# One fused two-layer kernel on one core: the opening, the compression tiles, the gated output and two norms reordered

## What is computed

```python
h = rmsnorm(x, norm_w)                                   # layer 1
proj = h @ w_in                                          # 16 column groups of 512 and more
kc, vc = compress(kc_raw, pe_k, w1_k, w2_k), compress(vc_raw, pe_v, w1_v, w2_v)
o = nsa_attention(q, kc, vc, ks, vs, kw, vw, gates)      # three branches, gated per head
y_b = (o * silu(g_nsa)) @ w_nsa_out
merged = gm[0] * y_a + gm[1] * y_b
x = rmsnorm(x + merged @ w_out, final_norm_w)
# layer 2: adaptive norm, attention a and b, gated merge
x = x + g1 * (merged @ w_out_2)
h2 = rms_norm(x, norm2_w) * (1 + sc2) + sh2
x = rms_norm(x + g2 * ff(h2), final_w)
```

## Time and profile before

| | |
|---|---|
| median of three runs | 2280.42 us (2279.46 to 2280.89) |
| profiled execution | 2282.75 us, its span 2281.1 us |
| TensorE busy | 2250.8 us, 99% of the span |
| VectorE, ScalarE, GpSimd busy | 1556.1, 1105.4, 149.9 us |
| data moved | 546.49 MB, 240 GB/s on average |
| share of TensorE in the chain that ended last | 87% |

### The profile page before, as it was taken

One profiled execution on the slowest core, in us unless ns is written; L12 is line 12 of the kernel. 1 busy time (PEld: TensorE's weight loads), 2 busy tenths in 40 slices (PEclk: granted clock), 3 DMA queues, 4 the chain that ended last, 5 costly groups with the idle time before them and its releaser, 6 DMA issues.

```text
span 2281.1 us, 31278 instructions
## 1 busy us (share of the span) xinstructions
PE 2250.8 (99%) x10377; PEld 1863.9 (82%) x10377; DVE 1556.1 (68%) x1936; ACT 1105.4 (48%) x1437; POOL 149.9 (7%) x285
## 2 busy tenths in 40 slices
PE   8999999999999999999999999999999999999998
PEld 6888888788788888888888888888888888888886
DVE  5685777777776556788777776666555666655566
ACT  6454445566564444533366554445444443444444
POOL 1000110000000000011011210000000000000000
PEclk9999999999999999999999999999999999999999
DMA  8887897555665766598588886666666666666564
GB/s 286 288 283 266 302 337 253 205 193 202 211 225 175 272 209 228 199 320 292 195 284 288 311 317 248 235 217 213 210 212 221 230 222 228 227 213 208 207 205 146
DMA packets 150104, 546.49 MB, mean 240 GB/s; under 512 B 17249, under 2 KB 17392, under 8 KB 148496
## 3 DMA queue, kind: packets, MB, share of 16 engines
q1 hardware_dynamic: 112400, 406.37, 51.4%
q0 software_dynamic: 34752, 129.71, 16.3%
q10 hardware_dynamic: 2880, 9.44, 1.0%
HBM read 534.92 MB, written 10.53 MB: 239 GB/s over the span
## 4 chain that ended last, share of the span: by engine, by line
PE 87%; DVE 6%; ACT 3%; issue 2%; DMA 2%; DVEq 0%; ACTq 0%; SPq 0%
PE ps L1805 22%; PE ps L1807 22%; PE ps L1806 22%; PE ps L1922 5%; PE ps L1924 5%; PE ps L1923 5%; DVE w_lo L1065 2%; PE ps L1844 2%; DMA raw<-ws_dram 2%; ACT prob L787 1%; ACT w_hi L619 1%; PE ps L1981 1%; PE ps L2028 1%; DVE prob L1226 1%; PE ps L1822 0%
## 5 line engine op out<-in xcount | busy, mean ns | idle before, releaser
L1065 DVE TENSOR_TENSOR w_lo<-raw,w_hi 128x1024 fp32r<-128x1024 f32 x761 | 927.8, 1224 | 617.5 <-ACT w_hi L619 599.7
L619 ACT ACTIVATE w_hi<-raw 128x1024 fp32r<-128x1024 f32 x753 | 795.7, 1061 | 996.5 <-PE ps L1807 859.8
L1805 PE MATMUL ps<-w_hi,a_hi 128*128 128x512 f32 x1632 | 638.6, 391 | 3.4 <-DVE w_lo L1065 1.7
L1807 PE MATMUL ps<-w_hi,a_lo 128*128 128x512 f32 x1632 | 636.2, 390 | 0.0
L1806 PE MATMUL ps<-w_lo,a_hi 128*128 128x512 f32 x1632 | 636.0, 390 | 0.0
L1805 PEld LDWEIGHTS ps<-w_hi,a_hi 128*128 128x128 f32 x1632 | 306.9, 188 | 67.1 <-issue 2.2
L1807 PEld LDWEIGHTS ps<-w_hi,a_lo 128*128 128x128 f32 x1632 | 306.9, 188 | 64.1
L1806 PEld LDWEIGHTS ps<-w_lo,a_hi 128*128 128x128 f32 x1632 | 307.1, 188 | 63.1
L1922 PE MATMUL ps<-w_hi,a_hi 128*128 128x512 f32 x640 | 258.5, 404 | 0.4 <-DVE w_lo L1065 0.4
L1924 PE MATMUL ps<-w_hi,a_lo 128*128 128x512 f32 x640 | 249.8, 390 | 0.0
L1923 PE MATMUL ps<-w_lo,a_hi 128*128 128x512 f32 x640 | 249.3, 390 | 0.0
(11 more groups left out here) (310 smaller groups left out, 2125.4 us busy)
## 6 DMA issues: line engine op xcount, KB each, us to landing
raw<-ws_dram SPq DMA_DIRECT2D x769, 512.0 KB, 4.2
ada<-wa_dram POOLq DMA_DIRECT2D x192, 512.0 KB, 4.8
gates_spill<-gst ACTq DMA_DIRECT2D x16, 512.0 KB, 5.4
ga<-gates_spill POOLq DMA_DIRECT2D x8, 512.0 KB, 4.2
gb<-gates_spill POOLq DMA_DIRECT2D x8, 512.0 KB, 6.0
bias_c<-b_merge_dram POOLq DMA_DIRECT2D x9, 256.0 KB, 4.9
x<-x_dram SPq DMA_DIRECT2D x4, 512.0 KB, 7.6
cb<-c_dram POOLq DMA_DIRECT2D x2, 1024.0 KB, 5.1
```

The costliest lines, as they stand in the source:

```text
L619: act.activation(w_hi[:, k.slot(RING), :], raw[:, k.slot(RING), :], ACT.Copy).then_inc(hi_done, 1)
L1065: dve.tensor_tensor(w_lo[:, k.slot(RING), :], raw[:, k.slot(RING), :], w_hi[:, k.slot(RING), :].bitcast(F32), ALU.subtract).then_inc(lo_do ...
L1805: pe.matmul(o, hi(m, tb), w_hi[:, s, cols], start=m == 0, stop=False)
L1807: mm = pe.matmul(o, lo(m, tb), w_hi[:, s, cols], start=False, stop=m == of * kts - 1)
```

## The change

There are four independent parts.

**1. Opening.** The identity and norm weights are one tensor `first`, issued by SP ahead of everything. The first weight tile comes in two halves, the first piece of x in two halves on ACT's queue. ACT runs a tiny activation first. TensorE runs 11 matmuls on zeros (128x128), then the first turn, then seven more, then the first tile in two halves with turn 1 between and turn 2 behind; ACT and DVE split the first tile in halves, after the first `a_hi` and `a_lo`.

**2. Compression tiles.** `cmp_w1_k` alternates with `vw`, `cmp_w1_v` with the second q projection (before it followed `vw`), in the order of `BESIDE`. The transposes of the hidden rows and the last products of the compression stand later.

**3. Gated output.** In each nsa group DVE makes the gated output of the third unit ahead of that step's splits. The modulation that stood ahead of the splits goes behind the `y_lo` of that unit.

**4. Norms.** Tiles 2 to 7 of the last output chunk are dealt by block, tile 3 from its ring slot, the other five from outside the ring. The split of the next stage's tile 3 waits until tile 3's second half is used.

```diff
+BESIDE = [(1, 0), (1, 1)] + [t for j in range(6) for t in ((0, j), (1, j + 2))] + [(0, 6), (0, 7)]
...
+        HELD = RING - 1
+        ASIDE = [j for j in range(T_K - len(spots["norm2"]) - 1, T_K) if j != HELD]
+        WHOLE = ASIDE[0]
...
+            sp.dma_start(first[:], t["first"]).then_inc(first_in, 16)
+            sp.dma_start(raw[:, 0, 0:NC], ws[0][:, 0:NC]).then_inc(raw0_in, 16)
+            sp.dma_start(raw[:, 0, NC:TW], ws[0][:, NC:TW]).then_inc(raw_landed[0], 16)
...
+            act.dma_start(x0[:, 0, :, 0:S], x_first[:, :, 0:S]).then_inc(x0_in, 16)
+            act.dma_start(x0[:, 0, :, S:NC], x_first[:, :, S:NC]).then_inc(x_in[0], 16)
...
                 last_squares(name, 0)
                 std(name, 0)
+                split_after(At(kp + HELD), kp - T_K + WHOLE + 1)
                 round_hi(0)
...
-                        if nsa_ and j % 2:
-                            m = 3 * (j // 2) + 2
-                            modulation(ada0 + m, m)
+                        if nsa_ and j == 1:
+                            modulation(ada0 + 2, 2)
...
+                        if j == nu - 1:
+                            gated(u0 + (j - 1), *a.units[j - 1])
...
+                    if nsa_ and j == nu - 1:
+                        modulation(ada0 + 5, 5)
...
                 round_lo(0)
+                split(At(kp + HELD))
                 dve.wait_ge(tile_used, kc + T_K)
                 add(1)
...
-                for j in range(RING):
+                for j in range(WHOLE):
                     tile(kc + j, pair(gc), j, T_K, ah, al)
...
+            idle_turns(11)
+            pe.wait_ge(first_in, 16)
...
             x_turn(0)
-            x_turn(1)
-            for j in range(T_K):
+            idle_turns(7)
+            pe.wait_ge(t_free, TG["norm1"] + 3)
+            for q in range(2):
+                if q:
+                    pe.wait_ge(lo_done, 1)
+                else:
+                    pe.wait_ge(half0_lo, 1)
...
-            hidden(0)
-            project("vw")
-            turn_hidden(0)
-            hidden(1)
+            hidden_beside("cmp_k_vw", 0, G0["cmp_k"])
```

More of the change, by code:

```diff
@@ L892, in _ @@
                 act.activation(gates[:, tb], ps[:, 7, tb * 3 * NQ:(tb + 1) * 3 * NQ], ACT.Sigmoid, scale=rstd[:, tb:tb + 1])
-            project("q01", 7, 1)
+            hidden(1)
+            evict(7, At(G0["q1"]), ACT.Copy)
+            project("qup", 8, 0)
+            hidden_turned(1)
+            project("qup", 9, 1)
             act.wait_ge(cmp_done, 2)
             act.activation(vc[:], ps[0:N_CMP, 5, :], ACT.Copy).then_inc(cmp_ready, 1)
[L896 to L899, removed]
+            for c in range(2, 4):
+                project("qup", 8 + c, c)
             for c in range(2):
@@ L1524, in _ @@
                 else:
-                    for m in range(RING):
-                        split_aside("norm2", At(k + RING + m), m)
+                    for m in range(WHOLE, T_K):
+                        if m == HELD:
+                            split(At(k + m))
+                        else:
+                            split_aside("norm2", At(k + m), ASIDE.index(m))
                 if c:
@@ L2035, in _, with idle_turns @@
                 pe.sem_inc(a.pv_done, 1)
-            pe.wait_ge(first_in, 32)
+            pe.wait_ge(zeros_in, 1)
+            def idle_turns(n):
+                for _ in range(n):
+                    pe.matmul(ps[:, 7, 0:P], squares[:, 1, 0:P], squares[:, 1, 0:P], start=True, stop=True)
+            idle_turns(11)
+            pe.wait_ge(first_in, 16)
             def x_turn(r):
-                if r % 2 == 0:
+                if r == 0:
+                    pe.wait_ge(x0_in, 16)
+                elif r == 1 or r % 2 == 0:
                     pe.wait_ge(x_in[r // 2], 16)
@@ L2046, in _ @@
             x_turn(0)
-            x_turn(1)
-            for j in range(T_K):
+            idle_turns(7)
[3 more added lines that the diff above has]
+                    pe.wait_ge(lo_done, 1)
+                else:
+                    pe.wait_ge(half0_lo, 1)
+                cols = slice(q * NC, (q + 1) * NC)
+                for tb in range(TB):
+                    out = pair(g)[:, tb, :]
+                    pe.matmul(out, ah(q, tb), w_hi[:, 0, cols], start=q == 0, stop=False)
+                    pe.matmul(out, ah(q, tb), w_lo[:, 0, cols], start=False, stop=False)
+                    mm = pe.matmul(out, al(q, tb), w_hi[:, 0, cols], start=False, stop=False)
+                if q == 0:
+                    x_turn(1)
+            mm.then_inc(tile_used, 1)
+            x_turn(2)
+            for j in range(1, T_K):
                 pe.wait_ge(t_free, TG["norm1"] + j + 3)
@@ L2055, in project, with hidden_beside @@
                 gemm(At(T0[name] + n * T_K), At(G0[name] + n), ah, al, T_K)
-            def hidden(n):
-                name = ("cmp_k", "cmp_v")[n]
+            def hidden_beside(phase, n, g):
                 pe.wait_ge(kb_ready, n + 1)
-                gemm(At(T0[name]), At(G0[name]), lambda m, tb: kb_hi[:, m, :], lambda m, tb: kb_lo[:, m, :], 8,
-                     kts=4, rows=CMP_ROWS, blocks=1, width=CMP_H)
+                pe.wait_ge(acc_free, g + 1)
+                for k, (of_kb, j) in enumerate(BESIDE):
+                    if of_kb:
+                        tile(At(T0[phase] + k), pair(At(g)), j, 8, lambda m, tb: kb_hi[:, m, :],
+                             lambda m, tb: kb_lo[:, m, :], kts=4, rows=CMP_ROWS, blocks=1, width=CMP_H)
+                    else:
+                        if j == 0:
+                            pe.wait_ge(acc_free, g + 2)
+                        tile(At(T0[phase] + k), pair(At(g + 1)), j, T_K, ah, al)
             def turn_hidden(n):
@@ L2111, in _ @@
                 mm.then_inc(cmp_done, 1)
[L2112 removed]
+            with pe.Fori(1, 3) as i:
                 for c in range(2):
```

164 lines of the change are left out of this document (99 added, 65 removed).

## The result

| kernel | median of the runs | ratio to before, 95% interval |
|---|---|---|
| before | 2280.91 us (2279.46 to 2281.54, 6) | |
| after | 2289.39 us (2287.32 to 2293.59, 6) | 1.0040 [1.0028, 1.0053] |

The change makes the kernel 8.5 us slower; 12.9 us faster were forecast, and the time lies outside the range. The profiled execution of after took 2293.59 us (span 2291.9, mean granted clock 0.994, against 0.999 before).

The account below looks back on a forecast made before the run. TensorE was taken as the bound, busy 2250.8 of 2281.1 us, leaving some 30 us of idling or half pace. Opening 4.4, compression 3.5, gated output 4.8 and norms 0.2 made 12.9 us: 2267.5 us, range 2263.0 to 2273.0.

Parts of the forecast that it names:

- The step that failed: End of each nsa group: the 1.24 us wait for `pcT` goes in four groups; 4.8 us gained, ends 0 and 5.0.
- The clock behind a wait: Opening: matmuls take 0.43 us at the low clock, 0.23 at the high; the clock was taken to rise within tile 0.
- The opening: Kernel start: the second weight tile begins at 13.2 us instead of 17.59; 4.4 us gained, ends 0 and 5.8.
- The 18 matmuls on zeros themselves: Opening: at 0.25 us each they take 2.8 and 1.8 us, ending before what they would delay is there.
- the cover: Opening: slack between the matmuls on zeros and what they could delay, 0.6 us at the first and 0.5 at the second.
- The landing of x: Opening: the first bytes (`first` and half the first x piece) land at 5.4 us, bounds about 4.9 and 7.1.
- The compression: Compression tiles: alternating with projection tiles removes all three waits for `w_lo`; 3.5 us gained, ends 2.4 and 3.9.
- The norms: Norm2 loses 0.8 us, norm3 gains 1.0; together 0.2 us gained, ends -2.5 and 2.7.
- the second trouble: Norm2: a second wait for `xn`, about 1.2 us, at the third turn, which comes 1.1 us later.
- (c): Nsa groups: the `pcT` wait becomes one for the next group's turned q; gated output gives 0, 2272.3 us; chance 0.08.
- (d): Norms: the ring runs dry in the dealt chunks, deciding from copies of 6.4 us; 2287.9 us; chance 0.03.
- the falsifier: Nsa groups: the forecast is wrong if a wait appears there that the waits listed before the change don't have.

Follow-up runs that it names:

- e8: The kernel before with the gated-output part alone, and the gate's bias load issued ahead of the group's last weight load; 2276.30 us.
- e2: The kernel after with the first gate bias load of a group issued ahead of its last modulation weight load on GpSimd's queue; 2271.17 us.
- e1: The kernel after with modulation 5 of each group put back ahead of the splits; 2275.80 us.
- e9: The kernel after with the gate's bias issued ahead of the last weight load, but behind the same wait for the modulation; 2285.27 us.
- e10: The kernel after with modulation 5 back ahead of the splits and the bias load ahead of the group's last weight load; 2271.55 us.
- e12: The kernel after with 18 idle matmuls ahead of TensorE's wait at the start of each nsa group; 2292.06 us.
- e15: The kernel before with the norms part alone; 2281.61 us.
- e3: The kernel before with the gated-output part alone, as changed; 2296.28 us.

## Why the prediction was wrong

- **The step that failed** is in part 3: "behind it on DVE are the two splits ... Next late is the copy of the second half of the probabilities", and "The 1.24 us goes in each of four groups". It names what stands behind the moved instructions on VectorE and what TensorE waits for, but leaves out who waits for the moved modulation: GpSimd's load, and behind that load, in the same queue, the gate's bias. The forecast had 4.8 us gained; it is 4.8 gained (e8) and 18.2 lost (after against e2, medians). The miss is 2289.4 - 2267.5 = 21.9 us, and all of it but 3.7 us is this.
- **The clock behind a wait** had a term in the opening alone. A new wait of 4 to 5 us had to be priced with it; it is a third of the loss here (7.2 of 21 us).
- **The opening**: 3.1 us for 4.4. The clock came as taken (0.23 us a matmul from the first). The mis-sized term was "The 18 matmuls on zeros themselves (0.25 each, 2.8 and 1.8 us)": a turn is two records, the first eleven took 5.0 us at the slow pace, and the cover of "0.6 us" was not there. The landing of x was off too, 5.4 for 6.5 (7.3 in after's trace), so the two errors hid each other. Of the forecast 4.4 us, 0.24 was a misreading: the chain's row 17.59 begins behind the start of the second tile, which the timeline has at 17.35. `first` has 72 KB, not 74.
- **The compression**: 2.9 us for 3.5, inside its ends. The waits went as described.
- **The norms**: 0.2 forecast, -0.7 and -1.0 measured, both within what is measured as nothing. At norm2 the first turn's wait stayed (1.5 us for 1.4), as argued; the second trouble was two waits of 0.25 and 0.33 us where one of 1.2 was said, though the third turn came 7.46 us behind the first for 6.49 before, near the 1.1 us forecast. Norm3 in after had one wait of 0.64 us for 0.6, at a copied tile instead of the third turn, and none at its first turn. That this fits is partly luck: in e1, e9, e2 and e10, with the same norms, norm3's first turn waited 0.7 to 1.8 us.
- **The rivals**: (c) had the right place, a new wait that takes over from `pcT` at the next group's start, but the wrong cause, and put a floor under it at nothing gained. It came about in small in e1 (0.7 us three times). The slower rival (d) was not it: no wait for the dealt tiles exceeds 0.64 us, and the weight tiles sent for between 928 and 950 us of after's trace took 4.7 us to land (median of nine), where it needed 6.4. The range was too low because each rival of part 3 stopped at zero. What saved the reading was the falsifier: "if a wait appears in the groups that rows 2 don't have".

## What to carry to other kernels

For each instruction that a change moves, list every engine that waits for its semaphore and what stands behind that wait in that engine's queue, transfers first; then compare each transfer's issue with the new time of its reader, since a faster engine uses up the lead as surely as a later issue. A load with no need of a wait should not stand behind one that has it. And price a new TensorE wait of several microseconds above its length, by the matmuls that run at half pace behind it.

## What the runs showed of the hardware

- Waits of TensorE of 4.15, 4.61 and 4.99 us (after) lowered the granted clock to 0.50 to 0.52 for the 12 matmuls behind each. Matmuls whose result nobody reads kept it at 1.00 (e12).
- Of waits of 2 to 3 us some lowered it and some did not: 2.17 us (e8, in the compression; 0.52 in the 3.5 us from 177.6, which is 1.2 us behind it), 2.96 us (e15, later attention; 0.53 in the 3.6 us behind it) and 3.08 us (e9) did, 2.92 and 2.95 us (e9) did not.
- The granted clock reads 1.00 from the start of the span, yet the first idle turns took 0.227 us a record and those after the turn of x 0.124 (14 in 1.73 us). In the opening the pace of the records tells the level and the clock's column does not.
- The same 256 KB load took 3.6, 5.2, 7.1 and 8.5 us to land (e2, before, e9, after). In the 1.4 us ahead of its issue in e2 and the 2.2 us in before the DMA engines moved nothing; in the 2.2 us ahead of it in after their share was 0.92.
- The same code between norm2's first and norm3's last turn took 615.5 us in before's trace and 612.6 in e3's: single traces differ by 3 us in a stretch that nothing changed.
